# Decay and beta rows by transfer, and sample states' products in column groups, in a hybrid decoder layer

## The reference, cut to what matters

```python
def gated_delta_chunked(q, k, v, g, beta, state):
    # Per token: S <- exp(g) S; S <- S + k (beta (v - S^T k))^T; o = S^T q.
    ...
    gc = jnp.cumsum(g, axis=-1)
    decay_incl = jnp.exp(jnp.where(incl, gc[..., :, None] - gc[..., None, :], -jnp.inf))
    decay_strict = jnp.where(strict, decay_incl, 0.0)
    kb = k * beta[..., None]
    a_mat = jnp.einsum('bhncd,bhnjd->bhncj', kb, k) * decay_strict
    rhs = jnp.concatenate([v * beta[..., None], kb * jnp.exp(gc)[..., None]], axis=-1)
    sol = lax.linalg.triangular_solve(a_mat + jnp.eye(c, dtype=a_mat.dtype), rhs, ...)
    value, k_cum = sol[..., :dv], sol[..., dv:]
    qk = jnp.einsum('bhncd,bhnjd->bhncj', q, k) * decay_incl
    ...
    def step(s, inp):
        val, kc, qk_c, qd, kd, gl = inp
        u = val - jnp.einsum('bhcd,bhde->bhce', kc, s)
        o = jnp.einsum('bhcd,bhde->bhce', qd, s) + jnp.einsum('bhcj,bhje->bhce', qk_c, u)
        s = s * gl[..., None, None] + jnp.einsum('bhcd,bhce->bhde', kd, u)
        return s, o
```

## Time and profile before

| | us |
|---|---|
| median of 3 runs | 3845.22 |
| lowest, highest | 3839.84, 3849.98 |
| the profiled execution | 3841.5 |
| its span, first to last instruction | 3839.8 |
| TensorE matmul busy (mean granted clock 0.837) | 3232.0 |
| VectorE busy | 1787.3 |
| ScalarE busy | 622.4 |
| GpSimd busy | 816.7 |

### The profile page before, as it was taken

How to read it: one execution, slowest core, us unless ns; L and a number is a source line. 1 busy time by engine, 2 the same in 40 slices (tenths; PEclk the granted TensorE clock), 3 DMA queues, 4 the chain that set the end, 5 groups by cost and what they waited for, 6 DMA issues and landing times.

```text
span 3839.8 us, 51087 instructions
## 1 busy us (share of the span) xinstructions
PE 3232.0 (84%) x18104; PEld 2209.3 (58%) x18104; DVE 1787.3 (47%) x4186; ACT 622.4 (16%) x1638; POOL 816.7 (21%) x921
## 2 busy tenths in 40 slices
PE   8999999999998899999899999978765666665564
PEld 7767777777776679999788888745410000000000
DVE  2396655555554310003633333358965444444544
ACT  1001222222221100001011110122221111111111
POOL 1000222211211000000122222223233333333332
PEclk9999999999999889999999999979865555555555
DMA  5433323323331358887799999999999999999997
GB/s 188 152 124 126 112 92 108 114 93 107 111 107 68 127 178 294 295 288 259 272 419 419 417 419 417 418 404 417 386 371 418 418 416 418 417 416 414 415 416 305
DMA packets 201143, 1089.73 MB, mean 284 GB/s; under 512 B 27088, under 2 KB 68944, under 8 KB 73616
## 3 DMA queue, kind: packets, MB, share of 16 engines
q0 software_dynamic: 92160, 671.13, 42.6%
q1 hardware_dynamic: 101760, 394.97, 28.9%
q10 hardware_dynamic: 7120, 22.22, 1.5%
HBM read 1056.59 MB, written 31.65 MB: 283 GB/s over the span
## 4 chain that ended last, share of the span: by engine, by line
PE 54%; DMA 29%; DVE 10%; issue 5%; ACT 1%; POOL 1%; DVEq 0%; SPq 0%; ACTq 0%; POOLq 0%
PE psum L497 24%; DMA branches<-in_peer_u,idx 24%; PE psum L561 15%; DMA ring<-in_peer_u,idx 4%; DVE branches L1801 2%; PE psum L921 2%; DVE branches L1355 2%; DVE ring L1801 1%; PE psum L634 1%; PE psum L643 1%; PE psum L640 1%; PE psum L739 1%; PE psum L338 1%; PE psum L620 1%; PE psum L904 1%
## 5 line engine op out<-in xcount | busy, mean ns | idle before, releaser
L1801 DVE CUSTOM_DVE_ANT_0 ring<-ring,psum 128x1024 f32<-128x1024 f32 x480 | 566.8, 1218 | 644.9 <-DMA ring<-in_peer_u,idx 602.8
L497 PE MATMUL psum<-hT,ring 128*128 128x128 f32 (+2 forms) x4800 | 802.5, 328 | 29.1 <-DMA ring<-in_w_glu 10.6
L497 PEld LDWEIGHTS psum<-hT,ring 128*128 128x128 f32 x4800 | 720.0, 196 | 104.0 <-issue 31.5
L904 PE MATMUL psum<-shared,selb 24*128 24x512 bf16 x1280 | 304.0, 524 | 460.8 <-DVE dots L1801 455.9
L904 PEld LDWEIGHTS psum<-shared,selb 24*128 24x128 bf16 x1280 | 56.5, 96 | 1025.9 <-DVE dots L1801 933.0
L561 PE MATMUL psum<-hT,ring 128*128 128x320 f32 x2112 | 626.4, 436 | 9.4 <-DMA ring<-in_w_att 7.8
L561 PEld LDWEIGHTS psum<-hT,ring 128*128 128x128 f32 x2112 | 382.9, 192 | 142.1 <-issue 15.2
L1215 ACT ACTIVATE ge<-dots 128x1 f32<-128x1 f32 x320 | 94.4, 295 | 1493.6 <-DVE dots L1801 1493.6
L497 PE MATMUL psum<-branches,ring 128*128 128x128 f32 (+1 forms) x2048 | 297.1, 304 | 6.4 <-ACT shared L1151 6.4
L1801 DVE CUSTOM_DVE_ANT_0 branches<-branches,psum 128x1024 f32<-128x1024 f32 x160 | 189.0, 1219 | 237.4 <-DMA branches<-in_peer_u,idx 236.0
L497 PEld LDWEIGHTS psum<-branches,ring 128*128 128x128 f32 x2048 | 287.6, 193 | 10.0 <-issue 10.0
(11 more groups left out here) (385 smaller groups left out, 3343.0 us busy)
## 6 DMA issues: line engine op xcount, KB each, us to landing
ring<-in_w_merge SPq DMA_DIRECT2D x160, 1024.0 KB, 5.2
ring<-in_w_head SPq DMA_DIRECT2D x64, 1024.0 KB, 4.9
ring<-in_w_outp SPq DMA_DIRECT2D x32, 1024.0 KB, 7.0
ring<-in_w_pq SPq DMA_DIRECT2D x32, 1024.0 KB, 8.2
ring<-in_w_att SPq DMA_DIRECT2D x24, 1024.0 KB, 5.5
ring<-in_w_mem SPq DMA_DIRECT2D x16, 1024.0 KB, 5.1
ring<-in_w_glu SPq DMA_DIRECT2D x16, 1024.0 KB, 6.5
out_qkv_out<-ring ACTq DMA_DIRECT2D x16, 520.5 KB
```

The source lines that it names most:

```text
L497: last = mat(out, ring[:, j, (k0 + kt) * P:(k0 + kt + 1) * P], src[:, kt, :], start=kt == 0, stop=kt == kts - 1)
L904: last = mat(ps[q][:, :], selb[32 * q:32 * q + 24, j, :], hb[32 * q:32 * q + 24, g_, :], start=True, stop=True)
L1801: v.tensor_tensor_reduce(out=u, in0=u, in1=x, scale=1.0, scalar=0.0, op0=ALU.mult, op1=ALU.add, accum_out=dots[:, g_, j, half_:half_ + 1]) ...
```

## The change

Five edits in the delta stage:
- The sample unit's 64 tokens lie in 128 slots: four groups of 32 columns, each with 16 tokens (two sequences) and 16 free. `slots(x)` and `sampled(x)` are the two views. Operations of VectorE on the whole row split in two for kn, qn and vv. L544's third unit is written in four groups of 16 rows, four matmuls for each of the 16 steps.
- Decay and beta rows: two sets of three small products, once for all heads, give 16 rows of 384 each; they go to a DRAM tensor `head_rows`, and SP brings each head's two rows back to all 128 partitions by one broadcast transfer (`decay_rows_in`), issued between weight tiles 1 and 2. L594, L596 and GpSimd's `gb`, `bb` go.
- Keys' and queries' products with the sample states become one set: group q of `knm` has 8 keys and 8 queries of two sequences, and eight matmuls with 32 weight columns write four column groups. They stand after level 1. `vb` is completed at level 2; ScalarE copies the result to `q_state` at level 3; a matmul with the identity's columns takes the queries' part to the output in L661's place.
- The queries' copies into `knm` stand on VectorE between `qn` and `tt`.
- `um` has four blocks instead of eight (two sequences share a block, in separate halves of the rows); L666 and L674 become two matmuls of 64 rows each behind `so_done`.

```diff
+            def decay_rows_in(h, used=True):
+                if used:
+                    sp.wait_ge(rows_used, 2 * h)
+                sp.dma_start(gb_rows, head_rows[h].partition_broadcast(P)).then_inc(gb_in, 16)
...
+            sp.wait_ge(sp_v, 4)
+            sp.dma_start(head_rows[:, :, :], gb_rows[0:H, :, :]).then_inc(rows_out, 16)
+            sp.wait_ge(rows_out, 16)
+            decay_rows_in(0, used=False)
             head_tiles(1, range(4))
             with sp.Fori(2, H) as h:
                 window_in(h - 1)
-                head_tiles(h, range(4))
+                head_tiles(h, range(2))
+                decay_rows_in(h - 1)
+                head_tiles(h, range(2, 4))
                 states_in_out(h - 1)
...
             for t in range(UNITS):
-                n = P if t < 2 else NS
                 for kt in range(KT):
-                    last = mat(ps[2][0:n, 32 * t:32 * t + 32], hT[:, kt, t * P:t * P + n], ab_w[:, 32 * kt:32 * kt + 32],
-                               start=kt == 0, stop=kt == KT - 1)
+                    for q in range(4 if t == 2 else 1):
+                        r0, n = (32 * q, 2 * TS) if t == 2 else (0, P)
+                        at_ = t * P + q * 2 * TS
+                        last = mat(ps[2][r0:r0 + n, 32 * t:32 * t + 32], hT[:, kt, at_:at_ + n], ab_w[:, 32 * kt:32 * kt + 32],
+                                   start=kt == 0, stop=kt == KT - 1, skip_group_check=t == 2)
...
+                    for u in range(UNITS):
+                        mat(ps[5][0:H, u * P:(u + 1) * P], gz[:, H * u:H * (u + 1)], mu3[:, u, :], start=True, stop=True)
+                    for u in range(UNITS):
+                        last = mat(ps[6][0:H, u * P:(u + 1) * P], sp3[:, 3, H * u:H * (u + 1)], ident[:], start=True, stop=True)
+                    last.then_inc(sp_b, 1)
...
-                fill(TOP)
-                pe.wait_ge(gb_ready, h1)
-                pe.wait_ge(sn_ready, h)
-                for u in range(UNITS):
-                    mat(ps[7][:, u * P:(u + 1) * P], gb[:, u, :], mu3[:, u, :], start=True, stop=True)
-                for u in range(UNITS):
-                    last = mat(ps[6][:, u * P:(u + 1) * P], bb[:, u, :], ident[:], start=True, stop=True)
-                last.then_inc(rows_done, 1)
-                fill(5)
+                fill(TOP + 5)
...
-                pe.wait_ge(rows_used, 2 * h1)
+                pe.wait_ge(sn_ready, h)
                 pe.wait_ge(v_ready, h1)
...
-                fill(4)
-                pe.wait_ge(knm_ready, h1)
-                pe.wait_ge(sin_in, 16 * h1)
-                pe.wait_ge(tok_read, 2 * h1)
-                for b in range(NBATCH):
-                    last = mat(ps[7][0:NS, 384:512], knm[:, b * NS:(b + 1) * NS], sin[:, b, :], start=b == 0, stop=b == NBATCH - 1)
-                last.then_inc(ks_done, 1)
-                fill(3)
+                fill(7)
...
+                    if l == 1:
+                        pe.wait_ge(knm_ready, h1)
+                        pe.wait_ge(sin_in, 16 * h1)
+                        pe.wait_ge(tok_read, 2 * h1)
+                        for c in two:
+                            for q in range(4):
+                                last = mat(ps[7][32 * q:32 * q + 32, 384:512], knm[:, c, 32 * q:32 * q + 32], sin[:, 2 * q + c, :],
+                                           start=c == 0, stop=c == 1, skip_group_check=True)
+                        last.then_inc(ks_done, 1)
...
-                mat(ps[5][:, 256:TOKENS], uu[:, 1, :], qkd[:, 2, 0:NS], start=True, stop=False, skip_group_check=True)
-                for b in range(NBATCH):
-                    c = slice(TP + b * TS, TP + (b + 1) * TS)
-                    mat(ps[5][:, c], sin[:, b, :], qn[:, c], start=False, stop=b == NBATCH - 1, skip_group_check=True)
+                mat(ps[5][:, 256:TOKENS], uu[:, 1, :], qkd[:, 2, :].rearrange("p (q n) -> p q n", q=4)[:, :, 0:2 * TS], start=True, stop=False, skip_group_check=True)
+                mat(ps[5][:, TP:TOKENS], q_state[:], queries_to_tokens, start=False, stop=True, skip_group_check=True)
                 pe.wait_ge(s1_ready, h1)
                 mat(ps[7][:, 2 * P:3 * P], kn[:, P:2 * P], s1, start=True, stop=True).then_inc(ks_done, 1)
-                pe.wait_ge(um_ready, h1)
-                umf = um.rearrange("p b e -> p (b e)")
-                mat(ps[6][:, :], kd[:, 2, :], umf[:, 0:512], start=True, stop=True).then_inc(sn_done, 1)
...
-                mat(ps[7][:, :], kd[:, 2, :], umf[:, 512:1024], start=True, stop=True).then_inc(sn_done, 1)
+                pe.wait_ge(um_ready, h1)
+                for q in two:
+                    r = slice(64 * q, 64 * q + 64)
+                    last = mat(ps[6 + q][:, :], kd[r, 2, :], um[r, :, :], start=True, stop=True)
+                last.then_inc(sn_done, 1)
...
+                    if l == 3:
+                        act.wait_ge(r_ready, 2 * h + 1)
+                        fn(q_state[:], ps[7][:, 384:512], ACT.Copy).then_inc(p_ready, 1)
...
-                dve.wait_ge(rows_done, h1)
+                dve.wait_ge(gb_in, 16 * h1)
...
                 v.tensor_tensor(qn, qn, egb[:], ALU.mult).then_inc(qd_ready, 1)
+                dve.wait_ge(qd_ready, h1)
+                for c in two:
+                    at_, to_ = slice(c * TS, (c + 1) * TS), slice((2 + c) * TS, (3 + c) * TS)
+                    last = v.tensor_copy(knm[:, c, :].rearrange("p (q n) -> p q n", q=4)[:, :, to_], slots(qn)[:, :, at_])
+                last.then_inc(knm_ready, 1)
                 dve.wait_ge(lt_ready, len(LEVELS) * h + 1)
...
+                    if l == 2:
+                        dve.wait_ge(tok_read, 2 * h1)
+                        dve.wait_ge(ks_done, 2 * h + 1)
+                        v.scalar_tensor_tensor(vb[:, 2, :], ps[7][:, 384:512], hs[:, NBEG + 2:NBEG + 3], vb[:, 2, :],
+                                               ALU.mult, ALU.add).then_inc(r_ready, 1)
...
-                g.tensor_tensor(um, uu[:, 1, :].unsqueeze(1).to_broadcast([P, NBATCH, P]),
-                                bm[:].unsqueeze(2).to_broadcast([P, NBATCH, P]), ALU.mult).then_inc(um_ready, 1)
+                g.tensor_tensor(um, uu[:, 1, :].unsqueeze(1).to_broadcast([P, 4, P]),
+                                slot[:, 0:4].unsqueeze(2).to_broadcast([P, 4, P]), ALU.mult).then_inc(um_ready, 1)
```

More of the change, by code:

```diff
@@ L182, in build @@
         qwin, qn, kn, vv = view(low, at, 3, QWIN), view(low, at, UT), view(low, at, UT), view(low, at, UT)
-        dt3, db3, gb, bb = (view(low, at, UNITS, P) for _ in range(4))
+        dt3, db3 = (view(low, at, UNITS, P) for _ in range(2))
+        gb_rows = view(low, at, 2, UT)
         at = [0]
         six = ring[:, 6, :]
-        sin, um = view(six, at, NBATCH, P), view(six, at, NBATCH, P)
+        sin, um = view(six, at, NBATCH, P), view(six, at, 4, P)
         at = [0]
         seven = ring[:, 7, :]
-        knm, qkd, tt, tn = view(seven, at, NBATCH * 72), view(seven, at, UNITS, P), view(seven, at, UNITS, P), view(seven, at, UNITS, P)
+        knm, qkd, tt, tn = view(seven, at, 2, P), view(seven, at, UNITS, P), view(seven, at, UNITS, P), view(seven, at, UNITS, P)
         zs = view(seven, at, TOKENS)
@@ L198, in build, with slots, sampled @@
         sqo = mean[:]
+        slot, q_state = sb("slot", [P, 5]), sb("q_state", [P, P])
+        queries_to_tokens = ident[:].rearrange("p (q n) -> p q n", q=4)[:, :, 2 * TS:]
+        def slots(x):
+            return x[:, TP:TP + P].rearrange("p (q n) -> p q n", q=4)[:, :, 0:2 * TS]
+        def sampled(x):
+            return x[:, TP:TOKENS].rearrange("p (q n) -> p q n", q=4)
         psum = ctx.enter_context(nc.psum_tensor("psum", [P, 8, 512], F32))
@@ L420, in _ @@
             window_in(H - 1)
+            decay_rows_in(H - 1)
             states_in_out(H - 1)
@@ L964, in _ @@
             act.wait_ge(ab_done, 1)
-            for u in range(UNITS):
-                n = P if u < 2 else NS
-                last = fn(ab[0:n, u, :], ps[2][0:n, 32 * u:32 * u + 32], ACT.Copy)
+            for u in two:
+                fn(ab[:, u, :], ps[2][:, 32 * u:32 * u + 32], ACT.Copy)
+            for q in range(4):
+                r = slice(32 * q, 32 * q + 2 * TS)
+                last = fn(ab[r, 2, :], ps[2][r, 64:96], ACT.Copy)
             last.then_inc(sp_a, 1)
@@ L1382, in _ @@
             st.wait()
-            st(v.memset(gz[NS:P, 32:48], 0.0))
+            st(v.tensor_tensor(slot[:, 0:4], bm[:, 0:4], bm[:, 4:8], ALU.add))
+            st(v.tensor_reduce(slot[:, 4:5], bm[:], AX, ALU.add))
+            st.wait()
+            st(v.tensor_scalar(gz[:, 32:48], gz[:, 32:48], slot[:, 4:5], None, ALU.mult))
+            st(v.tensor_scalar(sp3[:, 3, 32:48], sp3[:, 3, 32:48], slot[:, 4:5], None, ALU.mult))
             st.wait()
@@ L1434, in silu @@
                 dve.wait_ge(tanh_ready, 3 * h + j + 1)
-                out_ = cv[:, j, :] if j < 2 else vv[:, 0:TOKENS]
```

(16 more changed lines are left out.)

38 lines of the change are left out of this document (21 added, 17 removed).

## The result

| | us |
|---|---|
| median after, 4 runs (3779.31 to 3785.0) | 3782.68 |
| median before, on the same chips, 4 runs | 3847.09 |
| ratio, with its 95% interval | 0.9835 (0.9818 to 0.9852) |
| span after, profiled execution (before 3839.8) | 3780.2 |

The change takes 1.65% off. The page of the kernel after: busy us, share and instructions; shares of the chain of waits.

What follows compares the result with a forecast made beforehand. TensorE was taken to bound each head until other engines' chains came last; heads -41.2 and setup +5.4 us gave -35.8, so a median of about 3810 us. Own range 3798 to 3822, with A's middle and B 3786 to 3834.

Steps and rivals of the forecast that it cites:

- The bound: In a head: TensorE is busy for all 56.49 us, so matmuls taken out shorten it until another engine's chain comes last.
- (a): In each head: the decay and beta row products L594 and L596 go, 1.34 us a head.
- L668's wait: Without L661 and L666, L668 waits for VectorE's `vb`: 1.8 us a head gained, TensorE idle for 0.7.
- L673 to L626: From `so_done` to level 1: 1.7 us a head gained, the chain to `tt` ending last, each query copy waiting for one mask.
- Rival A: The query copies into `knm` aren't held up; a head gains 3.7 us up to L626, total 3790 us; chance 0.22.
- The key product: Behind level 1: eight matmuls in four column groups cost 1.1 us a head, bounds 0.7 and 2.0.
- (d): L666 joins L674 behind `so_done` as two 64-row products; that place gets 0.3 to 1.2 us longer, 0.3 taken.
- Setup: Before the heads: L544's third unit +4.1 us (0.06 a record), row products once for all heads +1.3, together +5.4.
- Head 15: Last head, TensorE at half clock at its end: 5.0 us gained in all, 4.3 of them up to L668.
- B: Narrow column groups run one behind the other: (b), the key product, takes 2.0 us, L544's third unit 14.1; 3830 us; chance 0.14.
- C: New gaps and small products let the granted clock fall within the heads: 4 us a head, 3870 us; chance 0.07.
- What was costed at nothing: Each head's broadcast, the states' load, the `q_state` copy and the sample unit's `vb` at level 2 cost no time.

Runs made afterwards that it cites:

- rows_back: Changed kernel with the decay and beta rows again made by L594's and L596's products in every head, no per-head transfer; 3800.81 us, ratio 0.9903.
- um_back: Changed kernel with `um` at eight blocks again, half multiplied in L666's old place, half behind `so_done`, with full rows; 3785.46 us, ratio 0.9856.
- um_wide: Changed kernel with only GpSimd's `um` product as wide as before (1024 elements), TensorE's work unchanged; 3787.46 us, ratio 0.9859.
- queries_back: Changed kernel with the queries' eight products of 8 moving columns back in L661's place, no query copies into `knm`; 3803.78 us, ratio 0.9906.
- copies_six: Changed kernel with four more copies of the same shape, read by nobody, behind the two query copies on VectorE; 3803.43 us, ratio 0.9898.
- copies_act: Changed kernel with the two query copies on ScalarE instead of VectorE; 3778.60 us, ratio 0.9835.
- groups_in_turn: Changed kernel with the same narrow matmuls reordered, one column group after the other, in L544's third unit and the heads; 3782.89 us, ratio 0.9847.
- fill_and_act: Changed kernel with the query copies on ScalarE and one fill moved before L689, into the wait for `vb`; 3764.03 us, ratio 0.9799.
- queries_filled: Changed kernel with the queries' eight narrow products back and one fill moved into the wait behind them; executions took 3796.2, 3793.3, 5415 and 10124 us.

## Why the prediction was wrong

**The bound.** Right. TensorE was the bound of a head, and its timeline gave the prices of what goes: (a) is 1.34 us in the prediction, 1.29 by rows_back.

**L668's wait, -1.8 a head.** Right in mechanism and size: 1.78 us from L681 to L689 instead of 3.54, with an idle time of 0.45 in the profile where 0.7 was forecast. The starts came as forecast (0.84 us from L681 to L687, 0.94 on to L689, against 0.86 and 0.9), so it is the counting of the idle time that differs: the profile takes it from L687's modelled end, 0.49 us behind its start. um_back and um_wide show the part that rests on GpSimd's shorter `um`: 0.48 us a head (the prediction had 0.6). queries_back shows that the queries' product gave 1.5.

**L673 to L626, -1.7.** The step that failed: -2.77 came. The reading that the chain from `so_done` through VectorE and GpSimd ends last there was right, and `at3` started 16.6 us behind `so_done` as forecast (16.7). The mis-sized term is the copies: "So I let each copy wait for one mask". They cost one mask together, `tt` ended 4.3 us behind `at3`'s start, not 5.3. From the rows of before I had seen that a narrow operation waits; that a second one passes with a first that has waited was in none of them, and I took the costlier reading as if there were nothing between it and no wait at all. That a mask more would have cost this much is shown by copies_six, where two more cost 1.39 us a head. Rival A (no wait), 3790 us, came nearer to the time than the forecast, but for a reason that didn't hold: it has TensorE bound by itself, and at one mask it nearly is (copies_act gained 0.31 us a head). A middle case, one mask, belonged among the cases. 1.07 us x 14 = 15 us.

**The key product, +1.1.** It was +0.77: the interval from level 1 to level 2 went from 4.16 to 4.93 us. 8 matmuls of half L712's columns took 0.58 us up to the next fill, 0.036 a record where 0.05 was taken, and 0.19 us went at their edges where 0.3 was taken. That is near the lower bound given (0.7). 5 us over the heads. (d) was as forecast: 3.10 us from L694 to L704 instead of 2.70, +0.4 for 0.3.

**Setup, +5.4.** It was +0.65. L571 by shape in the changed kernel, against the earlier trace rows:

```profile
L571 PE MATMUL psum<-shared,hT 128*16 128x32 f32 x128 | 1.9, 242 | 0.0
```

128 records of 16 weight columns took 1.9 us at half clock, 0.015 each, where I took 0.06 and held 0.03 for the lower end. The third unit got 1.7 us cheaper instead of 4.1 dearer. The bound from the nearest row, L712 with 256 moving columns, was no bound for 32. The products of the rows took 1.4 us (1.3 forecast). 5 us.

**Head 15, -5.0.** It was -8.75 in the profiled execution, and most of the difference is luck with the clock. The prediction kept the half clock of the kernel before at the end of head 15; in the changed kernel's trace it fell, within head 15, only behind `so_done`. It would be easy to say that the products that are gone (L661) had brought it down. The traces don't bear that out. In the kernel before the clock was at half from 1251.3 us, 0.9 before L661: L655 there already lasts 0.64 us instead of 0.39. And groups_in_turn, which has none of these products and the changed kernel's work in head 15, had half clock there. TensorE in the kernel before, then in the changed kernel, then in groups_in_turn, with the clock of the last two:

```profile
1251.07 0.64 PE L655 MATMUL psum<-mm 128*128 128x128 f32 x2 [0.47 <-ACT mm L1037]
...
1195.80 0.49 PE L689 MATMUL psum<-mm,ring 128*128 128x128 f32 x2 [0.45 <-DVE mm L1563]
...
1192.00:1196.00 4.00, 2.56 (x18) 2.00 (x17) 0.77 (x2) 0.66 (x2) 1.04 (x1) 1.00 0.00 0
...
1196.26 0.80 PE L681 MATMUL psum<-mm 128*128 128x128 f32 x2 [0.47 <-ACT mm L1067]
...
1199.20 0.80 PE L689 MATMUL psum<-mm,ring 128*128 128x128 f32 x2 [0.44 <-DVE mm L1563]
...
1196.00:1200.00 4.00, 3.30 (x12) 2.71 (x12) 0.35 (x1) 0.48 (x2) 1.04 (x1) 0.50 0.00 0
```

L681 to L689 takes 2.94 us in groups_in_turn and 1.8 in the changed kernel. From `so_done` of head 14 to the first product behind the heads groups_in_turn took 68.47 us, 5.4 less than the kernel before: with the half clock kept, as the prediction had it, its 5.0 came out about right. Of the nine traces without the eight products, three had the clock at half before head 15's `so_done` (copies_six and copies_act too), six didn't; of the three with them, all had. What decides it is open. 4 us of the 27.

**The rivals.** B (groups one behind the other) is out: L668 and L571 overlap. The drain that the Trainium skill describes ("TensorEngine Tiling (Array Packing)", "Key Properties") stays small here: a quarter of L620's 2.0 us is 0.5, level 1 got 0.77 us longer, so at most some 0.14 us are left for each of the two turns (an estimate), where 0.6 was the costly case. C (the clock falls in the heads) didn't happen in the heads of the changed kernel up to 14, where the clock is 1.00. In queries_back the products that the change removes, together with the gap that it makes, went with a fall of the clock in four heads.
The rule of the Trainium skill's page "SBUF — State Buffer", section "Who interferes with whom", that a VectorE copy in a two-port mode and a GpSimd operation exclude each other for the whole instruction, fits the first copy of each pair (0.86, 0.98 and 0.70 us, against 0.17 for the second). How many masks two copies wait for doesn't follow from it: the two masks were the prediction's own reading, and one was measured.

**What was costed at nothing** stayed so: no VectorE wait for the broadcast or the states appears in the heads.

The errors add up: 17 us in the steady heads with (d) and the key product, 5 in the setup, 4 in head 15, 1 in head 0, all to the same side: 62.9 us by the traces against 35.8 forecast. The copies had been set at their costly end; the key product and L571 had been set inside their bounds, and came out near the lower bound and below it; head 15's part is luck.

## What to carry to other kernels

Where VectorE and GpSimd meet, count in turns: a short VectorE operation waits for the GpSimd operation that runs, here every second one, and the length of a GpSimd operation that nobody needs yet can set the pace of TensorE; shorten it, or give the small copy to ScalarE. After matmuls are taken out, the waits that they covered come to light (0.45 and 0.2 us here by idle time, 0.89 by starts), and one fill moved into the longer one took another 0.54 us a head off, 8 us or 0.2%. (The ratios of fill_and_act and copies_act differ by 0.36%; the traces put some 3 us of that on where the clock fell around head 15.) Before a fall of the clock is put down to the instructions at it, look at where it began, and at other kernels with the same stretch. For a cost that depends on who waits for whom, list every count between none and the most, each with its own chance.

## What the runs showed of the hardware

- VectorE's copies of 128x32 elements beside GpSimd's masks: 0.70 to 0.98 us for the first of a pair, 0.17 for the second, six in a row passing as three pairs (copies_six).
- 128 records with 16 weight columns and 32 moving ones in four column groups: 0.015 us each at half clock; with the groups in turn 0.043 at half and 0.025 at full clock (groups_in_turn).
- Two 64-row products of 512 columns into two banks took 1.06 us together.
- Between heads 0 and 14 the granted clock fell to half in four heads behind 16 records of 8 moving columns and a gap of 0.44 us (queries_back), and in none with these records without the gap (queries_filled) or with the gap without them (the changed kernel); one execution each.
- In head 15, where TensorE has gaps of some 0.5 us at each level, the clock was at half before `so_done` in six of twelve traces, three of them without the narrow records.
